# Four small changes of order in a two-block kernel on one core: rounds, weights, swap tiles, taps

## The chip, the cores and the metric

The kernel runs on one core of a Trainium2 chip. The metric is the device time of one execution in microseconds. The core has five engines with a queue each: TensorE (PE, matmuls; its weight loads are PEld), VectorE (DVE), ScalarE (ACT), GpSimd (POOL) and SyncE (SP), which here only issues DMAs. They meet at semaphores; each engine runs its instructions in the order in which they were written.

## The reference

Two blocks on 1024 tokens of width 1024, in float32. The first block has two layers. Each: a norm; `z = hn @ w_in` (256 columns for a pooling mixer, then queries, keys and values of 12 heads of 64); a rotary turn of the first 16 of each head's 64 features; attention in three patterns of window and dilation, whose outputs are weighed by a softmax over their log sums; `w_out`; an FFN of width 4096 with a squared ReLU; a gated addition. The second block (`hybrid_layer`) is one layer:

```python
q, k, v, z_att, glu_a, glu_b, z_conv, g_att, g_conv = split(x @ w_in + b_in)
att_branch = (stick_breaking_attention(q, k, v) * silu(z_att)) @ w_att_proj
c = glu_a * sigmoid(glu_b)
c = silu(layer_norm(causal_depthwise_conv(c, conv_w, conv_b)))   # 31 taps, 512 channels
conv_branch = (c * silu(z_conv)) @ w_conv_proj + b_conv_proj
merged = sigmoid(g_att) * att_branch + sigmoid(g_conv) * conv_branch
y = layer_norm(ALPHA * x + merged @ w_out)
```

Stick breaking: the weight of key s for query t is `sigmoid(z)` times the product of `1 - sigmoid(z)` over all later keys before t, a running product along the keys.

## The kernel before, in words

Everything lies with features on partitions and tokens along the free axis, in two halves of 512 tokens. Each float32 product is three matmuls of rounded operands (`triple`, L1248 to L1250): high by high, low by high, high by low. The weights of a linear layer come in panels of 128 output features and 8 chunks of 128 input features. SP loads a panel into one of two slots of `w_raw` (`load`), POOL splits it into `w_hi` and `w_lo` (`split`, four operations, two for each half of the chunks), and PE runs it for both halves of the tokens (`half`, `half2`; 24 matmuls each). The first four halves of a layer run panel 0 and panel 1 on the first tokens, then both on the second. The order of work on every engine is written out by hand; side jobs are woven between PE's chunks by tables (`weave`, `weave2`), which put a job behind chunk k of half m.

**Start of a layer.** Panels 0 and 1 are the pooling input. PE then sums squares over features with a matmul by ones (L1298), ACT takes a root into `rstd`, DVE inverts it. POOL clears the rope tables and `swapped_rows` (`prepare`, L1087 to L1089; in layer 0 not before ACT has squared ten tiles), then SP loads the rope tables. Before the change, POOL's order is split 0, split 1, `prepare`, split 2, `attention_consts`, split 3. `PANELS` is 108 per layer.

**The rotary turn** (`take_qk`, `add_swapped`, `swap`). There are 6 units of a query, a key and a value panel. For each half of a query or key panel DVE writes bank times cosine to `q_t` or `k_t` (L2266) and bank times sine to the one tile `s_half` (L2270, which frees the bank); SP sends four small DMAs (L859, L860) from `s_half` to `swapped_rows`, with the two groups of eight rows exchanged; DVE adds `swapped_rows` (L2257). The add of one half stands ahead of the next write of `s_half`, so that the tile is free. The value panel goes to `v_feat` (L2277), in front of the last add; PE transposes it (`turn_v`, L1304) behind chunk 1 of the next unit's first half.

**Stick breaking** (`score`, `scan`, `turn_weights`, `meet`). Four pairs of heads, 12 rounds each of up to 512 keys (`ROUNDS`), and three steps more for lagging work. A round: PE scores (L1596), ACT makes `fail` and `weight` (L2075, L2076), POOL masks the diagonal, DVE scans (L2662, L2664) and multiplies (L2669), PE transposes two steps later (L1583), ACT copies, and PE multiplies by the values (`meet`, L1570). The rounds of pairs 0 to 2 stand 4 chunks apart, those of the last pair, beside the four panels of `z_att` (Z_ATT), 3 chunks. `take_z` gates the attention output, with `s_half` as its tile; `lower_weighed` splits it.

**The convolution** (`convolve`) is 124 taps on DVE (L2617, L2621), each a multiply and add over 1024 tokens. They are put between other work on DVE: one beside some of the rounds, eleven behind the last `lower_weighed`, and up to ten behind each gate panel of G_ATT.

**Gate panels** (`panel2`). From G_ATT on, a panel runs both halves into one of two pairs of banks; a panel of 8 chunks (a gate: ACT's `gate`, L2109, frees the bank) takes turns with one of 4 chunks (a projection: DVE's product, L2754, frees it). Four panels of Z_CONV lie between G_ATT and G_CONV; `branch_high` and `branch` prepare the convolution branch there.

Of the kernel before, what the change touches and what calls it, by code (L numbers as in the profile page):

```python
# [10 lines left out]
ALU = mybir.AluOpType  # L11
ACT = mybir.ActivationFunctionType

P = 128
# [50 lines left out]
def half_bank_no(no):  # L65

    l, m = divmod(no, HALVES)
    if l < DEPTH and m >= GATE_AT:
        return (6, 7, 0, 1, 2)[(24 * BLOCKS + m - GATE_AT) % 5]  # L70
    return (0, 1, 2, 6, 7)[m % 5] if m < (10 if l < DEPTH else 20) else m % 3
# [223 lines left out]
GLU, QKV, Z_ATT, G_ATT, Z_CONV, G_CONV, W_OUT2, PANELS2 = 0, 8, 20, 24, 40, 44, 60, 68  # L295
# [7 lines left out]
PAIRS = 4  # L303
# [18 lines left out]
def weave2():  # L322
    at = {}

    def put(m, k, *job):
        at.setdefault(m, []).append((k, job))

    put(0, 1, "stat", 0)
    put(1, 3, "stat", 1)
    for c in range(PAIRS):  # L330
        m0 = 2 * QKV + 6 * (c + 1)
        for b in range(2):

            k = 6 + b if c == PAIRS - 1 else 8 + b
            put(m0 + k // 8, k % 8, "turn_v2", c, b)
        for u in range(STEPS2 if c == PAIRS - 1 else len(ROUNDS)):
            k = 2 + (3 if c == PAIRS - 1 else 4) * u
            put(m0 + k // 8, k % 8, "stick", c, u)
    for m in at:
        at[m].sort(key=lambda x: x[0])  # L340
    return at
# [58 lines left out]
def two_blocks(nc, x, p, positions, norm1, w_in, pool_w, pool_scale, w_out, norm2, w_up, w_down,  # L400
# [39 lines left out]
    tmp = place("tmp", [P, HALF])  # L440
# [136 lines left out]
    ple_raw_loaded = sem("ple_raw_loaded")  # L577
    tables_stored = sem("tables_stored")
    rope_loaded = sem("rope_loaded")
    rows_swapped = sem("rows_swapped")  # L580
    spilled = [sem(f"spilled{k}") for k in range(KC)]
    reloaded = [sem(f"reloaded{k}") for k in range(KC)]
    stats_out = sem("stats_out")
# [129 lines left out]
    w_out2_d = w_out_2[0].rearrange("(k q) f -> q k f", q=P)  # L713

    ALL = DEPTH * PANELS
    ROTATIONS = 4 * UNITS
    STATS = 6

# [8 lines left out]
    def half_cols(hf):  # L727
        return slice(hf * HALF, hf * HALF + HALF)
# [69 lines left out]
    def _(sp):  # L798
# [55 lines left out]
        def swap(l, n, hf):  # L854

            sp.wait_ge(half_free, half_no(l, n, hf) + 1)
            cols = half_cols(hf)
            for at in (0, 64):
                sp.dma_start(swapped_rows[at:at + 8, cols], s_half[at + 8:at + 16]).then_inc(rows_swapped, 16)  # L859
                sp.dma_start(swapped_rows[at + 8:at + 16, cols], s_half[at:at + 8]).then_inc(rows_swapped, 16)  # L860

        def read_stats(l, c):
            sp.wait_ge(stats_out, 64 * (2 * l + c + 1))
# [100 lines left out]
    def _(pool):  # L964
# [164 lines left out]
        for l in range(DEPTH):  # L1129
            for n in range(PANELS):  # L1130
                if n in (GATE - 2 * UP + 3, GATE - 2 * UP + 5):
                    for c in range(2):
                        lower_p(l, c, (n - GATE + 2 * UP) // 2 - 1)
                if is_pair(l * PANELS + n):
                    split_pair(l * PANELS + n)
                elif l or n >= 2:
                    split(l * PANELS + n)
                if n == 1:
                    prepare(l)
                if n == 2:  # L1140
                    attention_consts(l)
                if 4 <= n < 10:
                    mixing(l, n - 4)
                if n >= GATE:
                    split_ple(l, n - GATE)
# [588 lines left out]
    def _(act):  # L1734
# [370 lines left out]
        def gate(m, col, func, dst=gate2[:]):  # L2105
            if m > G_ATT:
                act.wait_ge(slot_free, m - G_ATT)
            act.wait_ge(panel_done, m - G_ATT + 1)
            a.activation(dst, ring[m % 2][:], func, bias=bias2[:, col:col + 1]).then_inc(slot_free, 1)  # L2109
# [22 lines left out]
        for k in range(4):  # L2132
            act.wait_ge(ln_step, LN_SCALED1 + k)
            a.activation(conv_out[:, k], conv_out[:, k], ACT.Silu, scale=conv_par[:, 1, k:k + 1], bias=conv_par[:, 2, k:k + 1]).then_inc(ln_silued, 1)
        for f in range(4):
            if f >= 2:
                gate(Z_CONV + f, 24 + f, ACT.Silu, conv_in[:, f])
            branch_high(f)
        def merged_high(k):

# [24 lines left out]
    def _(dve):  # L2165
        v = nc.vector
# [84 lines left out]
        def add_swapped(l, unit, i, hf):  # L2251
            r, g = rotation(l, unit, i, hf), unit % GROUPS
            dst = half_pattern((q_t, k_t)[i][unit % 2][:], g, hf)
            dve.wait_ge(rows_swapped, 64 * (r + 1))
            dve.wait_ge(swap_cleared, l + 1)
            dve.wait_ge(scaled, r + 1)
            v.tensor_tensor(dst, dst, half_tokens(swapped_rows[:, half_cols(hf)], g), ALU.add).then_inc(rotated, 1)  # L2257

        def take_qk(l, unit, i, hf):
            no, g, cols = half_no(l, 2 + 3 * unit + i, hf), unit % GROUPS, half_cols(hf)  # L2260
            if unit < 2 and hf == 0:
                dve.wait_ge(spilled[2 + 3 * unit + i], 16 * (l + 1))
            if unit == 0 and i == 0:
                dve.wait_ge(roped, 4 * l + 2 * hf + 2)
            dve.wait_ge(half_done, no + 1)
            v.tensor_tensor(half_pattern((q_t, k_t)[i][unit % 2][:], g, hf), half_tokens(bank[half_bank_no(no)], g), half_tokens(rope_c[:, cols], g), ALU.mult)\  # L2266
                .then_inc(scaled, 1)
            if i or hf:
                add_swapped(l, unit, (2 * i + hf - 1) // 2, (2 * i + hf - 1) % 2)
            v.tensor_tensor(s_half[:], bank[half_bank_no(no)], rope_s[:, cols], ALU.mult).then_inc(half_free, 1)  # L2270

        def take_v(l, unit, hf):
            no, g, cols = half_no(l, 4 + 3 * unit, hf), unit % GROUPS, half_cols(hf)
# [409 lines left out]
        def take_z(f, hf):  # L2683
            no, cols, at = half2_no(Z_ATT + f, hf), half_cols(hf), 2 * f + hf
            dve.wait_ge(z_gated, at + 1)
            v.scalar_tensor_tensor(s_half[:], bank[half_bank_no(no)], bias2[:, 12 + f:13 + f], s_half[:], ALU.add, ALU.mult).then_inc(half_free, 1)
            dve.wait_ge(half_free, no + 1)
            dve.wait_ge(att_taken, 4 * f + 4)
            v.tensor_tensor(att2[:, f, cols], att2[:, f, cols], s_half[:], ALU.mult).then_inc(att_weighed, 1)
            if at:  # L2690
                lower_weighed(at - 1)
# [6 lines left out]
        for m in range(QKV, G_ATT):  # L2698
            for hf in range(2):
                for _, job in WEAVE2.get(2 * m + hf, ()):  # L2700
                    if job[0] == "stick":
                        if job[2] < len(ROUNDS):
                            scan(*job[1:])
                        c, u = job[1:]
                        if u < len(ROUNDS) and ROUNDS[u][2] == P or c < PAIRS - 1 and u in (1, 2):
                            convolve(1)
                if m < Z_ATT:
                    c, i = divmod(m - QKV, 3)
                    take_qkv(c, i, hf)
                    convolve(3 if c == 0 else 1 if i == 2 and hf else 0)  # L2710
                else:
                    take_z(m - Z_ATT, hf)
        lower_weighed(2 * PAIRS - 1)
        convolve(11)

        def branch(m, f, src, source):
            dve.wait_ge(slot_free, m - G_ATT + 1)
# [146 lines left out]
```

## Time and profile before

| | us |
|---|---|
| median of 3 runs (lowest, highest) | 3215.99 (3215.17, 3216.70) |
| the profiled execution's own time | 3214.32 |
| its span, first to last instruction | 3212.6 |
| PE busy | 3171.4 (99%) |
| DVE busy | 2030.2 (63%) |
| POOL busy | 1725.6 (54%) |
| ACT busy | 988.2 (31%) |
| mean granted clock of PE, share of full | 0.996 |

Busy time is the union of an engine's instructions. PE's matmuls overlap each other: one of 512 columns takes 390 ns in the profile and the next starts 227 ns after it. So what counts is when a matmul starts, and how long PE had no matmul before it.

### The profile page before, as it was taken

How to read it: one execution, taken by the hardware profiler on the slowest of the kernel's cores; microseconds unless marked ns; L12 is line 12 of the kernel's file. 1: busy time of each engine (PE TensorE's matmuls, PEld its weight loads, DVE VectorE, ACT ScalarE, POOL GpSimd, SP SyncE). 2: the span in 40 equal slices, each digit the busy share in tenths (PEclk: the TensorE clock that was granted, in tenths of full speed). 3: DMA queues.
4: the chain of work that ended last, by engine and by line, in shares of the span. 5: the costliest groups of instructions: out<-in, count | busy, mean ns of one | idle time of the engine just before them, and what ended most of it. 6: DMA issues, size and time to landing. Idle time of an engine off the chain costs nothing.

```text
span 3212.6 us, 39393 instructions
## 1 busy us (share of the span) xinstructions
PE 3171.4 (99%) x14756; PEld 2508.2 (78%) x14756; DVE 2030.2 (63%) x2749; ACT 988.2 (31%) x1847; POOL 1725.6 (54%) x1544
## 2 busy tenths in 40 slices
PE   8999999999999999999999999999999999999999
PEld 6676788888888887776788888888888766778887
DVE  6546576666666664545476666665758988797323
ACT  3222243333333421222253333332422244402212
POOL 5632356666666446532356666666455533386575
PEclk9999999999999999999999999999999999999999
DMA  5111211111112121111231111112111100011112
GB/s 151 48 40 34 84 55 53 53 53 53 55 50 63 50 87 55 45 40 45 71 58 53 53 53 53 55 53 66 45 46 46 40 27 27 21 46 50 49 54 85
DMA packets 306349, 173.73 MB, mean 54 GB/s; under 512 B 61424, under 2 KB 296944, under 8 KB 306160
## 3 DMA queue, kind: packets, MB, share of 16 engines
q1 hardware_dynamic: 287904, 162.55, 17.5%
q10 hardware_dynamic: 18256, 8.67, 0.9%
q8 instruction: 118, 1.93, 0.2%
q14 instruction: 71, 0.58, 0.1%
HBM read 155.13 MB, written 12.91 MB: 52 GB/s over the span
## 4 chain that ended last, share of the span: by engine, by line
PE 57%; DVE 2%; ACT 1%; issue 0%; POOL 0%; DMA 0%; SPq 0%; DVEq 0%; ACTq 0%; POOLq 0%
PE ring L1248 11%; PE ring L1249 11%; PE ring L1250 11%; PE aux L1248 3%; PE aux L1250 3%; PE aux L1249 3%; PE ring L1490 2%; PE ring L1491 2%; PE ring L1489 2%; PE aux L1596 1%; PE aux L1490 1%; PE aux L1489 1%; PE aux L1491 1%; PE aux L1570 1%; PE aux L1342 1%; PE aux L1328 1%
## 5 line engine op out<-in xcount | busy, mean ns | idle before, releaser
L996 POOL TENSOR_TENSOR w_hi<-w_raw,ones 128x512 fp32r<-128x512 f32 (+3 forms) x408 | 455.1, 1115 | 905.3 <-PE ring L1250 718.6
L999 POOL TENSOR_TENSOR w_lo<-w_raw,w_hi 128x512 fp32r<-128x512 f32 (+3 forms) x408 | 543.7, 1333 | 32.0
L1248 PE MATMUL ring<-Q_hi,w_hi 128*128 128x512 f32 x1312 | 519.8, 396 | 4.7 <-POOL w_lo L999 3.5
L1249 PE MATMUL ring<-Q_lo,w_hi 128*128 128x512 f32 x1312 | 511.8, 390 | 0.0
L1250 PE MATMUL ring<-Q_hi,w_lo 128*128 128x512 f32 x1312 | 511.7, 390 | 0.0
L1248 PEld LDWEIGHTS ring<-Q_hi,w_hi 128*128 128x128 f32 x1312 | 246.6, 188 | 82.2 <-issue 28.0
L1250 PEld LDWEIGHTS ring<-Q_hi,w_lo 128*128 128x128 f32 x1312 | 246.7, 188 | 52.1
L1249 PEld LDWEIGHTS ring<-Q_lo,w_hi 128*128 128x128 f32 x1312 | 246.8, 188 | 50.3 <-issue 1.0
L1248 PE MATMUL ring<-P_hi,w_hi 128*128 128x512 f32 x656 | 276.5, 422 | 1.2 <-DVE P_lo L2210 1.2
L1250 PE MATMUL ring<-P_hi,w_lo 128*128 128x512 f32 x656 | 257.7, 393 | 0.0
L1249 PE MATMUL ring<-P_lo,w_hi 128*128 128x512 f32 x656 | 257.7, 393 | 0.0
L1248 PE MATMUL aux<-Q_hi,w_hi 128*128 128x512 f32 x544 | 213.3, 392 | 0.0
L1250 PE MATMUL aux<-Q_hi,w_lo 128*128 128x512 f32 x544 | 211.8, 389 | 0.0
L1249 PE MATMUL aux<-Q_lo,w_hi 128*128 128x512 f32 x544 | 211.7, 389 | 0.0
L1933 ACT ACTIVATE aux<-tmp 128x512 f32<-128x512 f32 x112 | 67.4, 602 | 402.0 <-DVE tmp L2386 402.0
L2621 DVE SCALAR_TENSOR_TENSOR conv_out<-conv_in,taps,conv_out 128x1021 f32<-128x1021 f32 (+29 forms) x120 | 186.7, 1607 | 0.2
L1248 PEld LDWEIGHTS ring<-P_hi,w_hi 128*128 128x128 f32 x656 | 124.2, 189 | 48.6 <-issue 21.3
L1250 PEld LDWEIGHTS ring<-P_hi,w_lo 128*128 128x128 f32 x656 | 124.0, 189 | 27.9
L1249 PEld LDWEIGHTS ring<-P_lo,w_hi 128*128 128x128 f32 x656 | 124.5, 190 | 24.3 <-issue 2.9
L2284 DVE COPY probs_t<-aux 128x256 f32<-128x256 f32 (+1 forms) x96 | 52.4, 546 | 141.3 <-PE aux L1328 141.3
L1851 ACT ACTIVATE probs<-probs,neg_max 128x128 f32<-128x128 f32 (+1 forms) x192 | 85.1, 444 | 175.6 <-DVE neg_max L2296 175.6
L1023 POOL TENSOR_TENSOR w_lo<-w_sums,w_hi 128x1024 fp32r<-128x1024 f32 x56 | 134.5, 2401 | 0.0
(396 smaller groups left out, 7059.3 us busy)
## 6 DMA issues: line engine op xcount, KB each, us to landing
w_raw<-in_w_in SPq DMA_DIRECT2D x84, 512.0 KB, 3.8
w_raw<-in_w_up SPq DMA_DIRECT2D x64, 512.0 KB, 4.0
w_raw<-in_w_down SPq DMA_DIRECT2D x64, 512.0 KB, 3.4
h_scratch<-h ACTq DMA_DIRECT2D x16, 512.0 KB, 3.8
w_raw<-in_w_gate SPq DMA_DIRECT2D x16, 512.0 KB, 3.8
hx<-h_scratch SPq DMA_DIRECT2D x12, 512.0 KB, 6.5
x_raw<-in_x SPq DMA_DIRECT2D x8, 512.0 KB, 7.8
w_raw<-in_w_out SPq DMA_DIRECT2D x16, 256.0 KB, 2.9
```

The costliest lines, as they stand in the source:

```text
L996: g.tensor_tensor(w_hi[:, slot, ks], w_raw[:, slot, ks], one.broadcast_to([P, width, P]), ALU.mult).then_inc(w_hi_ready, 1)
L999: g.tensor_tensor(w_lo[:, slot, ks], w_raw[:, slot, ks], w_hi[:, slot, ks].bitcast(F32), ALU.subtract).then_inc(w_ready, 1)
L1023: g.tensor_tensor(w_lo[:, slot], w_sums[:, slot], w_hi[:, slot].bitcast(F32), ALU.subtract).then_inc(w_ready, 1)
L1248: t.matmul(o, wh, xh, start=first, stop=False)
L1249: t.matmul(o, wh, xl, start=False, stop=False)
L1250: return t.matmul(o, wl, xh, start=False, stop=last)
L1489: t.matmul(to[at], wh, xh, start=(i == 0 and not joins), stop=False, skip_group_check=True)
L1490: t.matmul(to[at], wh, xl, start=False, stop=False, skip_group_check=True)
L1491: mm = t.matmul(to[at], wl, xh, start=False, stop=(i == 1), skip_group_check=True)
L1851: a.activation(x_, x_, ACT.Exp, scale=SCALE, bias=neg_max[:, j % 2, e:e + 1], accum_out=row_stat[:, unit, j, 2 + e:3 + e]).then_inc(exped, 1)
L1933: a.activation(square_bank, tmp[:], ACT.Square).then_inc(squared, 1)
L2621: v.scalar_tensor_tensor(conv_out[:, c, shift:], conv_in[:, c, 0:S - shift], tap, conv_out[:, c, shift:], ALU.mult, ALU.add)\
```

## The change

Five edits. In `weave2` the last pair's rounds stand 4 chunks apart, as the others. On POOL `prepare` moves from behind split 1 to behind split 2. For unit 0 the second half's sine product goes to `tmp`, each half has its own semaphore `rows_swapped`, and the add stands behind the next sine product. ACT runs the gate of panel Z_CONV + 2 in front of the two first `branch_high`. Eight of the eleven taps behind `lower_weighed` move: one to round 7 of pairs 0 to 2, three to the last steps of the last pair, two behind `take_z` of the first two Z_ATT panels.

```diff
@@ weave2
-            k = 6 + b if c == PAIRS - 1 else 8 + b
+            k = 8 + b
             put(m0 + k // 8, k % 8, "turn_v2", c, b)
         for u in range(STEPS2 if c == PAIRS - 1 else len(ROUNDS)):
-            k = 2 + (3 if c == PAIRS - 1 else 4) * u
+            k = 2 + 4 * u
@@ two_blocks
-    rows_swapped = sem("rows_swapped")
+    rows_swapped = [sem(f"rows_swapped{hf}") for hf in range(2)]
+    def rotation_tile(unit, hf):
+        return tmp if unit == 0 and hf else s_half
@@ SP, swap
-            cols = half_cols(hf)
+            cols, scaled_half = half_cols(hf), rotation_tile((n - 2) // 3, hf)
             for at in (0, 64):
-                sp.dma_start(swapped_rows[at:at + 8, cols], s_half[at + 8:at + 16]).then_inc(rows_swapped, 16)
-                sp.dma_start(swapped_rows[at + 8:at + 16, cols], s_half[at:at + 8]).then_inc(rows_swapped, 16)
+                sp.dma_start(swapped_rows[at:at + 8, cols], scaled_half[at + 8:at + 16]).then_inc(rows_swapped[hf], 16)
+                sp.dma_start(swapped_rows[at + 8:at + 16, cols], scaled_half[at:at + 8]).then_inc(rows_swapped[hf], 16)
@@ POOL
-                if n == 1:
+                if n == 2:
                     prepare(l)
-                if n == 2:
                     attention_consts(l)
@@ ACT, behind the four Silu of the convolution branch
+        gate(Z_CONV + 2, 26, ACT.Silu, conv_in[:, 2])
         for f in range(4):
-            if f >= 2:
-                gate(Z_CONV + f, 24 + f, ACT.Silu, conv_in[:, f])
+            if f == 2:
+                gate(Z_CONV + 3, 27, ACT.Silu, conv_in[:, 3])
             branch_high(f)
@@ DVE, add_swapped
-            dve.wait_ge(rows_swapped, 64 * (r + 1))
+            dve.wait_ge(rows_swapped[hf], 64 * (r // 2 + 1))
@@ DVE, take_qk
-            if i or hf:
+            if unit and (i or hf):
                 add_swapped(l, unit, (2 * i + hf - 1) // 2, (2 * i + hf - 1) % 2)
-            v.tensor_tensor(s_half[:], bank[half_bank_no(no)], rope_s[:, cols], ALU.mult).then_inc(half_free, 1)
+            v.tensor_tensor(rotation_tile(unit, hf)[:], bank[half_bank_no(no)], rope_s[:, cols], ALU.mult).then_inc(half_free, 1)
+            if unit == 0 and (i or hf):
+                add_swapped(l, unit, (2 * i + hf - 1) // 2, (2 * i + hf - 1) % 2)
@@ DVE, stick breaking and behind it
-                        if u < len(ROUNDS) and ROUNDS[u][2] == P or c < PAIRS - 1 and u in (1, 2):
+                        if u >= len(ROUNDS) or ROUNDS[u][2] == P or c < PAIRS - 1 and u in (1, 2, 7):
                             convolve(1)
...
                     take_z(m - Z_ATT, hf)
+                    if hf and m - Z_ATT < 2:
+                        convolve(1)
         lower_weighed(2 * PAIRS - 1)
-        convolve(11)
+        convolve(3)
```

## Rows read from the trace of the kernel before

**Rows 1.** PE's waits, whole run: line, releaser, us in total, times, longest.
```profile
PE ring L1304 <- DVE v_feat L2277: 9.9, 2, 5.0
...
PE aux L1248 <- POOL w_lo L999: 5.0, 1, 5.0
PE aux L1583 <- DVE weight L2669: 3.6, 4, 2.4
PE ring L1248 <- POOL w_lo L999: 3.5, 1, 3.5
PE ring L1248 <- ACT conv_in L2109: 1.2, 1, 1.2
```

**Rows 2.** Stretches: length, busy of PE, PEld, DVE, ACT, POOL, clock, DMA, GB/s.
```profile
47.00:52.00 5.00, 4.58 (x14) 3.67 (x15) 4.22 (x7) 3.38 (x6) 4.46 (x8) 0.66 0.96 351
89.00:95.00 6.00, 5.93 (x18) 4.96 (x19) 1.05 (x1) 0.71 (x2) 5.84 (x5) 0.51 0.14 28
...
2768.00:2780.00 12.00, 8.70 (x52) 6.42 (x52) 9.13 (x9) 4.38 (x8) 1.19 (x1) 1.00 0.08 23
...
2815.00:2820.00 5.00, 4.77 (x14) 3.79 (x15) 5.00 (x3) 0.00 (x0) 4.92 (x4) 0.66 0.00 0
...
1278.00:1284.00 6.00, 5.43 (x20) 4.55 (x21) 1.53 (x2) 0.91 (x2) 5.43 (x5) 0.60 0.12 23
```

**Rows 3.** Timeline, PE in layer 0: start, length, operation, [idle before, releaser].
```profile
47.42 0.77 PE L1248 MATMUL aux<-P_hi,w_hi 128*128 128x512 f32 x1 [5.03 <-POOL w_lo L999]
...
57.84 1.02 PE L1298 MATMUL ring<-sumsq,ones 128*128 128x512 f32 x2
```

**Rows 4.** Timeline, POOL in layer 0: first clearing, last `w_lo` of panel 2.
```profile
42.20 0.96 POOL L1087 MEMSET rope_s<- 128x1024 f32 x1 [21.16 <-ACT aux L1770]
...
48.35 1.29 POOL L999 TENSOR_TENSOR w_lo<-w_raw,w_hi 128x512 fp32r<-128x512 f32 x1
```

**Rows 5.** Timeline, DVE in layer 0: last add of squares.
```profile
51.77 0.69 DVE L2205 TENSOR_TENSOR sumsq<-aux,sumsq 128x512 f32<-128x512 f32 x1 [0.26 <-ACT aux L1770]
```

**Rows 6.** Timeline, DVE in layer 1: rotary turn of unit 0.
```profile
1259.81 0.67 DVE L2270 TENSOR_TENSOR s_half<-aux,rope_s 128x512 f32<-128x512 f32 x1
...
1264.53 0.69 DVE L2257 TENSOR_TENSOR q_t<-q_t,swapped_rows 128x512 f32<-128x512 f32 x1 [3.45 <-DMA swapped_rows<-s_half]
...
1277.16 1.27 DVE L2277 TENSOR_TENSOR v_feat<-aux,rstd 128x512 f32<-128x512 f32 x2
```

**Rows 7.** Timeline, SP in layer 1: the load behind the first swap.
```profile
1263.22 0.44 SPq L847 DMA_DIRECT2D w_raw<-in_w_in  x1
```

**Rows 8.** Timeline, PE in layer 1: sum of squares, first transposes.
```profile
1247.47 1.02 PE L1298 MATMUL ring<-sumsq,ones 128*128 128x512 f32 x2
...
1278.57 1.08 PE L1304 MATMUL ring<-ident,v_feat 128*128 128x128 f32 x4 [4.87 <-DVE v_feat L2277]
```

**Rows 9.** Last pair: PE's longest wait; two stretches, last pair, pair before.
```profile
2771.68 0.66 PE L1583 MATMUL aux<-ident,weight 128*128 128x128 f32 x4 [2.42 <-DVE weight L2669]
...
2718.00:2776.00 58.00, 54.53 (x307) 36.25 (x307) 52.43 (x51) 35.30 (x61) 21.57 (x17) 1.00 0.08 23
...
2655.00:2717.00 62.00, 61.84 (x341) 42.54 (x341) 51.01 (x47) 30.62 (x54) 25.20 (x20) 1.00 0.09 26
```

**Rows 10.** Timeline, gate panels of G_ATT: DVE, POOL and PE.
```profile
2799.86 13.08 DVE L2621 SCALAR_TENSOR_TENSOR conv_out<-conv_in,taps,conv_out 128x1011 f32<-128x1011 f32 x11
...
2923.03 1.21 DVE L2754 TENSOR_TENSOR merged<-ring,gate 128x1024 f32<-128x1024 f32 x1
...
2806.46 7.37 POOL L996 TENSOR_TENSOR w_hi<-w_raw,ones 128x512 fp32r<-128x512 f32 x1 [7.67 <-PE ring L1250]
...
2844.46 1.10 POOL L996 TENSOR_TENSOR w_hi<-w_raw,ones 128x512 fp32r<-128x512 f32 x1 [4.39 <-PE ring L1250]
...
2925.75 0.39 PE L1248 MATMUL ring<-branch_hi,w_hi 128*128 128x512 f32 x1
```

**Rows 11.** Timeline, ACT: the second copy of the convolution branch.
```profile
2977.45 1.06 ACT L2113 ACTIVATE branch_hi<-conv_out 128x1024 fp32r<-128x1024 f32 x1 [3.43 <-DVE conv_out L2718]
```

## The prediction

> **What bounds the kernel.** I read the list of who waited for whom on TensorE first. TensorE (PE) is the engine that is nearly always busy in the profile's table, so a change can only win where PE stands still, or runs slowly after it stood still. The list has few lines [rows 1]: PE waits for `v_feat` at the transposes of L1304 (9.9 us, one wait of 5.0 and one of 4.9 in the two layers), once for POOL's weights in the first stage (5.0), four times for DVE's `weight` in stick breaking (3.6), once more for POOL's weights at the start of the gate panels (3.5), once for ACT's gate (1.2). 
>
> **Part 1, third panel's weights in front of the clearing.** In layer 0 POOL stands from 21 to 42.20 for ACT's squares before it may clear the tables, and only then splits panel 2, the last `w_lo` from 48.35 [rows 4]; PE, done with panel 1 at 42.2, restarts at 47.42 [rows 3]. In the new order the split waits only for PE's third half, whose last matmul starts 24 matmuls (5.5 us) and a sum of features (about 1 us) before 42.2, so near 35.5. The split takes what it takes here, 49.6-44.9 = 4.7 us, ends near 41 (42 if DVE's operations hold it), and its first half is ready near 38.5. The wait is gone with its slow stretch: 5.0+1.5 = 6.5 us. What is late next: the second sum of squares (L1298) stands at 57.84 [rows 3] and would now come at 51.3, but DVE's last add of squares ends at 51.77+0.69 = 52.46 [rows 5], and that chain (ACT square, DVE add, in turn) doesn't hang on PE. New wait 1.2 us. Besides, DVE's small angle operations at 39 to 41.5 now lie beside POOL's last `w_lo` (1.3 us): between 0 and 1.3 us later for the whole DVE chain, I take 0.5. Net gain 6.5-1.2-0.5 = 4.8, bounds 4.0 and 5.3. The clearing starts at 42.2 as before, since ACT's squares release it, so the rope loads on SP, and the load of panel 4 behind them, stay where they are; panel 4 is run two panels (four halves of 5.5 us) behind panel 2, from 64 on, and its load, issued by 53 behind the rope tables, and its split of 4.7 us end before that. POOL's constants and the split of panel 3 move up by the 4.7 us. In layer 1 the clearing moves from idle time to behind the split (2.7 us); SP's four rope loads and the load of panel 4 queue behind it and move with it. Nobody on PE's side waits: the tables are first read 6.4 us after L1298, PE needs panel 3 some 10 us later than it is split. Zero, with 0 to 1 us of loss as bounds.
>
> **Part 2, two tiles to swap from.** Today each rotated half is a closed circle: `s_half` at 1259.81, four DMA issues on SP, landing, the add at 1264.53, and only then the next `s_half` [rows 6]; three circles of 4.7 to 5.9 us stand before `v_feat` at 1277.16, done at 1278.4, and PE's transposes start at 1278.57 after 4.9 us of waiting [rows 8], so PE arrived at 1273.6. With a second tile the next product doesn't wait and SP's queue sets the pace: a swap's issues end where SP issues the load of weights behind it, at 1263.22 (0.44 us) [rows 7], 2.7 us after `s_half` was written, and the add follows 1.3 us later. Swap 2 then goes at 1263.7 to 1266.4 and lands at 1267.7; swap 3 goes at 1266.4 to 1269.1 and lands at 1270.5 (its product needs the add at 1264.53 only); DVE adds it until 1271.3 and writes `v_feat` twice, 1.2 us: 1272.5, with 0.14 to PE 1272.7. PE comes at 1273.6. So `v_feat` is ready 0.9 us early and the wait goes whole; swap 4 is added near 1275, and PE needs that some 6 us after its transposes. From L1298 to the transposes PE takes 1273.6-1247.47 = 26.1 us [rows 8] and DVE 25.2, and layer 0 has the same distances since both its chains hang on L1298. Gain in layer 0: 5.0+2.7 (the start-to-start distances behind it give 2.5, the clock row 2.9) = 7.7; in layer 1 4.9+2.0 = 6.9. If every add were stretched by POOL (0.6 to 1.2 us, three of them), 1 us of wait comes back in each layer.
>
> **Part 3, rounds four chunks apart.** All four waits of the 3.6 us lie in the last pair, the longest, 2.42 us, at 2771.68. In its rounds DVE is busy 52.4 of 58 us; in the pair before, with rounds four chunks apart, 51.0 of 62, and PE waits nowhere [rows 9]. A chunk is three matmuls, 0.68 us; over the last pair's twelve steps PE takes 12 of them more, and 3.3 us of waiting less: 58-3.3+8.2 = 62.9 us, for DVE's 52.4 and two moved taps of 1.2: 54.8. That is 87% where the pair before has 82% and no wait. Gain 3.6; at worst 1.5 of it stays. The last meet comes 14 chunks later, in the last half of the stage; `att_ready` is needed 5 chunks and a 10.9 us panel after it, DVE and ACT need about 7: hidden.
>
> **Part 4, taps spread.** Behind the stage DVE runs eleven taps back to back (2799.86, 13.08 us); POOL's `w_hi` starts at 2806.46 inside them and takes 7.37 us, until the taps end [rows 10]; PE waits 3.5 [rows 1]. With three taps (3.6 us) DVE is idle from 2803.5, POOL's split ends at 2806.46+4.7 = 2811.2, its first half at 2808.9, and PE wants it at 2811.7. Gain 3.5+1.6 = 5.1. The eight taps moved (1.2 us each) go into rounds with idle DVE time and to round 7 of three pairs, where two rounds of lag absorb 1.2 us. What is late next: the product `merged` of the seventh gate panel, 2923.03, ends 1.5 us before PE starts the panel that needs its bank at 2925.75 [rows 10]. DVE's tap series restart from PE's fourth panel in both versions, so this slack should stay; I take 0.2 off. 4.9.
>
> The Trainium skill, "SBUF — State Buffer", section "Who interferes with whom", says that a VectorE operation with two SBUF inputs and a GpSimd operation lock each other out for one whole instruction. By that the `w_hi` would have lasted one tap and itself, 2.3 us, and PE wouldn't have waited, so moving taps would win nothing there; the row of 7.37 us says that it was held through six taps, and I go by the row.
>
> **Part 5, ACT's gate for panel Z_CONV+2 earlier.** Now it runs at 2978.4, behind two copies; ahead of the second ACT waits 3.43 us for DVE, from 2974.0 [rows 11], and the gate needs 1.1. Ahead of both copies it is done by 2974, 4 us before PE asks for the bank. Gain 1.2. The first copy slips 0.2 us; its reader comes 10 us later.
>
> **Sum.** 4.8+7.7+6.9+3.6+4.9+1.2 = 29.1. The profiled execution took 3214.3 (span 3212.6 and 1.7 around it), giving 3185.2; it lies 1.7 under the median, so I predict **3187**. If every residue is nothing: 3186.
>
> The Trainium skill, "TensorE: Matmul & The Clock Gate", section "HAM oscillation — how this bites in real kernels", says that a wait can throttle the engine again. The rows agree for waits from 3.5 us and not for 2.4 [rows 2]; if the new wait did it, rival (a2) below is the time.
>
> **Rivals.** (a) As above, 3187, 3184 to 3191: 0.68. (a2) The new wait at L1298 sets the clock back as the four long ones do; it is shorter than the 2.4 us that didn't, but stands on its own: 1.5 us, 3188.5, 0.04. (b) DVE becomes late in the tap series: PE gets ahead of it by the 5.1 us it no longer loses, and the slack of 1.5 us at 2925.75 is eaten; for it, DVE is never idle over five panels there; against it, its series restarts at PE's fourth panel. A wait of 3.6 and 1.6 of slow clock: 3192. 0.10. (c) The swap still binds: the small copies issued behind a 512 KB load land with it, 3 us later than I put them; for it, both share SP's queue; against it, the circles after such a load are no longer today. A wait of 2 to 3 us per layer stays, 3187+5 = 3192. 0.09. (d) The taps don't hold POOL, something else did, or they hold it in another place: the change doesn't do what it says in part 4, 3192. 0.05. (e) Slower. The hold of POOL is not rare but comes whenever a split meets a tap series; five series of ten taps run through the gate panels, and the shifted start lets each meet the split of the next. Each hold costs up to 6.3 us at PE and 1.6 of clock, 7.9; three leave 5 us of the gain, from four on the kernel is slower; all five: 3187+5x7.9 = 3226. For it only the one hold; against it, a split that starts inside a series at 2844.46 takes 1.10 us [rows 10]. 0.02. (f) Small losses in several places, together over 20 us, within 0.2% of no change: 0.02.
>
> **Range.** (a) with (b) to (d): 3183 to 3195 holds over 8 in 10. A measurement here tells about 0.2% (6.4 us) from no change. Faster 0.96 ((a) to (d)), same 0.02 (f), slower 0.02 (e).
>
> **What would show it.** In the list of PE's waits L1304, L1583 and both L1248 lines behind `w_lo` gone, a new one of 1 to 2.5 us at L1298 behind `sumsq`; POOL's clearing in layer 0 still at 42; `v_feat` 1 us ahead of L1304; POOL's `w_hi` at the first gate panel 1.0 us; granted clock 1.00 in all four stretches. Wrong if L1304 still waits over 2 us, or if the gate panels show new waits.

## The result

Four runs of the changed kernel took 3191.18 to 3192.55 us, median **3191.8**; the kernel before took 3216.0 beside them (3215.17 to 3216.70). The ratio is 0.9925 with a 95% interval of 0.9908 to 0.9942: 24.2 us faster, where 29.1 were forecast. 3191.8 lies in the range given (3183 to 3195) and is 4.8 us above the value forecast, 3187. (The change has five parts; the title leaves out the fifth, ACT's gate.) The profiled execution took 3191.67 us (span 3189.9), 22.65 under that of before.

The profile after, first PE's waits (line, releaser, us in total, times, longest), to be read against [rows 1]:

```profile
PE aux L1409 <- DMA x_raw<-in_x: 7.2, 1, 7.2
PE ring L1302 <- DVE sumsq L2210: 3.8, 1, 3.8
PE aux L1587 <- DVE weight L2676: 2.2, 3, 1.7
PE aux L1332 <- ACT probs L1855: 1.6, 3, 1.1
PE ring L1252 <- DVE P_lo L2215: 1.2, 2, 0.7
PE ring L1360 <- DVE weights L2334: 0.6, 2, 0.3
PE ring L1252 <- DVE pool_u L2251: 0.5, 1, 0.5
```

The lines are four further down than before: L1302 was L1298, L1308 was L1304, L1587 was L1583, L1332 was L1328. Gone are the waits for `v_feat` (9.9), both for POOL's `w_lo` (5.0, 3.5) and the one for ACT's gate (1.2). The first line, for x, was there before. Three are over 1 us larger than forecast: 3.8 us at the second sum of squares (1.2 forecast), 2.2 us at L1587 (0 forecast), 1.6 us for `probs` (0.5 before, no change forecast). The clock in the stretches of [rows 2] and behind the new wait (length, busy of PE, PEld, DVE, ACT, POOL, clock, DMA, GB/s):

```profile
47.00:52.00 5.00, 4.54 (x19) 3.12 (x17) 4.54 (x8) 1.95 (x4) 4.68 (x6) 1.00 0.53 142
56.00:60.00 4.00, 4.00 (x10) 2.66 (x10) 1.77 (x1) 1.97 (x2) 0.00 (x0) 0.57 1.07 392
1278.00:1284.00 6.00, 6.00 (x31) 4.30 (x32) 5.59 (x14) 1.38 (x5) 4.95 (x5) 1.00 0.03 6
```

The slow stretches of before are at full clock; one has come in their place, 56 to 60 us at 0.57, which costs (1-0.57)x4 = 1.7 us.

Where the time came from is read from the start of the same matmul in both traces (the n-th matmul of L1248 before and of L1252 after; there are 3200 in each):

| up to | before | after | difference | this part | forecast |
|---|---|---|---|---|---|
| behind the second sum of squares, layer 0 | 60.79 | 60.40 | -0.4 | part 1: 0.4 | 4.8 |
| behind the transposes of `v_feat`, layer 0 | 96.84 | 88.56 | -8.3 | part 2: 7.9 | 7.7 |
| the same in layer 1 | 1292.72 | 1278.62 | -14.1 | part 2: 5.8 | 6.9 |
| behind stick breaking | 2792.55 | 2776.81 | -15.7 | part 3: 1.6 | 3.6 |
| second gate panel | 2819.67 | 2798.58 | -21.1 | part 4: 5.4 | 4.9 |
| last input panel of the convolution | 2979.65 | 2957.15 | -22.5 | part 5: 1.4 | 1.2 |

So of the 6.5 us that are missing between the profiles (29.1 less 22.65) 4.4 lie in part 1, 1.1 in layer 1 and 2.0 in part 3, together 7.5; parts 2 (layer 0), 4 and 5 gave 0.9 more than forecast, and 0.1 came behind the last row. One profile tells such a shift to about 1 us: in four more profiles with the order of before in the first stage (the kernel before with part 3, 4 or 5 alone, and the old order below) the matmul of the first row stands 0.2 to 1.1 us later than 60.79.

**Part 1.** DVE in layer 0 (start, length, operation, count, [idle before, releaser]):

```profile
39.63 1.15 DVE L2188 TENSOR_SCALAR turns<-ang 128x64 f32<-128x64 f32 x1
40.82 0.19 DVE L2190 TENSOR_SCALAR turns<-turns 128x64 f32<-128x64 f32 x1
...
42.32 1.81 DVE L2199 TENSOR_SCALAR turns<-turns 128x64 f32<-128x64 f32 x1
44.16 3.35 DVE L2235 RECIPROCAL rstd<-rstd 128x512 f32<-128x512 f32 x1
...
54.97 0.69 DVE L2210 TENSOR_TENSOR sumsq<-aux,sumsq 128x512 f32<-128x512 f32 x1 [0.75 <-ACT aux L1774]
```

and POOL and PE beside it:

```profile
39.39 1.34 POOL L1004 TENSOR_TENSOR w_lo<-w_raw,w_hi 128x512 fp32r<-128x512 f32 x1
42.23 0.96 POOL L1092 MEMSET rope_s<- 128x1024 f32 x1 [1.50 <-ACT aux L1774]
43.12 0.96 POOL L1093 MEMSET rope_c<- 128x1024 f32 x1
```

```profile
55.81 1.31 PE L1302 MATMUL ring<-sumsq,ones 128*128 128x512 f32 x2 [3.81 <-DVE sumsq L2210]
```

An operation of 0.19 us takes 1.15 and ends at 40.78, as POOL's `w_lo` ends (40.73); another takes 1.81 and ends at 44.13, as the second memset ends (44.08). The first pushed the second into the clearing, which DVE had been through with before. The last add of squares ends at 55.66; before it was 52.46 [rows 5].

**Layer 1.** PE doesn't wait for `v_feat`, but 1.1 us for `probs`. DVE, POOL and PE:

```profile
1273.45 2.40 DVE L2303 TENSOR_SCALAR neg_max<-row_stat 128x2 f32<-128x2 f32 x1
```

```profile
1273.43 2.39 POOL L1076 TENSOR_TENSOR pool_u<-mix,pool_u 128x1024 f32<-128x1024 f32 x1
```

```profile
1276.82 0.44 PE L1332 MATMUL aux<-ident,probs 128*128 128x128 f32 x2 [1.13 <-ACT probs L1855]
```

The same scaling of two numbers per row takes 0.17 us elsewhere. PE has come nearer to DVE by the wait it lost, and what stood in the shadow of that wait now stands in its way: with the wait back (one tile, below) PE waits 0.5 us for `probs`, as before.

**Part 3.** The end of the last pair in DVE, then POOL and PE:

```profile
2746.92 2.04 DVE L2628 SCALAR_TENSOR_TENSOR conv_out<-conv_in,taps,conv_out 128x1010 f32<-128x1010 f32 x1
2748.88 3.43 DVE L2671 TENSOR_TENSOR_SCAN left<-fail,not_yet 128x512 f32<-128x512 f32 x2
...
2762.96 3.91 DVE L2669 TENSOR_TENSOR_SCAN left<-fail,left 128x511 f32<-128x511 f32 x2 [0.23 <-DVE weight L2676]
2767.00 1.78 DVE L2676 TENSOR_TENSOR weight<-weight,left 128x1024 f32<-128x1024 f32 x1
```

```profile
2761.60 2.02 POOL L1159 TENSOR_TENSOR w_hi<-w_raw,ones 128x512 fp32r<-128x512 f32 x1 [3.03 <-PE ring L1254]
...
2767.78 2.13 POOL L1162 TENSOR_TENSOR w_lo<-w_raw,w_hi 128x512 fp32r<-128x512 f32 x1
```

```profile
2768.84 0.66 PE L1587 MATMUL aux<-ident,weight 128*128 128x128 f32 x4 [1.71 <-DVE weight L2676]
```

From the tap to the product at 2767.00 DVE is idle for no more than 0.23 us at a time, between its own operations. The scans at 2762.96 lie beside POOL's split of the output weights and take 3.91.

### The profile page after: what moved, and what is told of

It is laid out like the page before. It is cut to its first block, busy times and chain, and to the rows that moved or that the text cites. A ratio compares the mean times of both kernels' runs of the same rounds, so it can differ in the third digit from the quotient of the medians.

```text
span 3189.9 us, 39393 instructions
## 1 busy us (share of the span) xinstructions
PE 3164.3 (99%) x14756; PEld 2503.5 (78%) x14756; DVE 2036.2 (64%) x2749; ACT 988.1 (31%) x1847; POOL 1719.1 (54%) x1544
## 4 chain that ended last, share of the span: by engine, by line
PE 95%; DVE 4%; ACT 1%; issue 0%; DMA 0%; DVEq 0%; ACTq 0%; SPq 0%
PE ring L1252 18%; PE ring L1254 17%; PE ring L1253 17%; PE aux L1252 5%; PE aux L1254 5%; PE aux L1253 5%; PE ring L1495 3%; PE ring L1494 3%; PE ring L1493 3%; PE aux L1493 2%; PE aux L1494 2%; PE aux L1495 2%; PE aux L1346 1%; PE aux L1332 1%; PE aux L1322 1%; PE aux L1600 1%
## 5 line engine op out<-in xcount | busy, mean ns | idle before, releaser
L1001 POOL TENSOR_TENSOR w_hi<-w_raw,ones 128x512 fp32r<-128x512 f32 (+3 forms) x408 | 448.3, 1099 | 917.4 <-PE ring L1254 735.5
L1252 PE MATMUL ring<-Q_hi,w_hi 128*128 128x512 f32 x1312 | 519.2, 396 | 0.0
L1252 PEld LDWEIGHTS ring<-Q_hi,w_hi 128*128 128x128 f32 x1312 | 246.2, 188 | 76.4 <-issue 26.3
L1252 PE MATMUL ring<-P_hi,w_hi 128*128 128x512 f32 x656 | 275.8, 420 | 1.6 <-DVE P_lo L2215 1.2
L1252 PE MATMUL aux<-Q_hi,w_hi 128*128 128x512 f32 x544 | 213.3, 392 | 0.0
L1252 PEld LDWEIGHTS ring<-P_hi,w_hi 128*128 128x128 f32 x656 | 123.4, 188 | 49.3 <-issue 21.3
```

Source lines behind the costliest of these rows:

```text
L1001: g.tensor_tensor(w_hi[:, slot, ks], w_raw[:, slot, ks], one.broadcast_to([P, width, P]), ALU.mult).then_inc(w_hi_ready, 1)
L1252: t.matmul(o, wh, xh, start=first, stop=False)
```

## The experiments

All of them were timed in five rounds against the kernel before. Three base kernels occur: the one before, the changed one, and the changed one with the angles early. The median of the kernel before was 3215.0 to 3216.1 us in the four sets of runs, so a difference between times of two sets is good to about 1 us.

**Where part 1 went.** The angle operations moved into a gap of DVE, from 20 us:

```
             lower(P_hi, P_lo, gains[:, 0, 0], KC - 1, hf, KC * hf + KC - 1)
+            if hf == 0:
+                angles()
         for k in range(KC):
...
-        angles()
         for l in range(DEPTH):
```

> The changed kernel (3191.8 us) with DVE's ten small angle operations moved from behind the first sum of squares (39.1 to 44.1 us of the span) to the gap between the two halves of x (from 20 us). Theory: the 4.8 us that the third panel's weights were to bring were lost because the one-input ones among them stood until POOL's operation in flight was over (1.15 and 1.81 us for 0.20 each), and the chain behind them made TensorE wait 3.8 us for sumsq and then run 3.4 us at the half clock. Then the reciprocal starts at about 41 and not 44.2, the wait for sumsq falls from 3.8 to 0.5 to 1.2, the low clock behind it goes, and the time is 3186 to 3188. Rival 1: the squares are held back by ACT's own issues of the spills (1.6 and 1.5 us long), whatever comes before: the wait falls by 1 us at most, 3190 to 3191. Rival 2: the ten operations hold the second half of P back and TensorE with it: 3192 or more.

Measured 3187.12 (3185.65 to 3187.46), ratio 0.9912 (0.9898 to 0.9925), 4.7 us under the changed kernel, with no run of the one inside the other's. Its waits, one row of DVE, one of PE, one stretch:

```profile
PE aux L1587 <- DVE weight L2677: 2.2, 3, 1.7
PE ring L1252 <- DVE P_lo L2215: 1.2, 2, 0.7
PE aux L1332 <- ACT probs L1855: 1.1, 2, 0.8
PE ring L1302 <- DVE sumsq L2210: 0.9, 1, 0.9
```

```profile
40.92 3.35 DVE L2237 RECIPROCAL rstd<-rstd 128x512 f32<-128x512 f32 x1 [1.94 <-ACT rstd L1786]
```

```profile
52.02 1.10 PE L1302 MATMUL ring<-sumsq,ones 128*128 128x512 f32 x2 [0.94 <-DVE sumsq L2210]
```

```profile
56.00:60.00 4.00, 4.00 (x19) 3.31 (x18) 3.96 (x6) 0.00 (x0) 0.00 (x0) 1.00 0.54 151
```

The reciprocal starts 3.24 us earlier, the wait is 0.9 where 3.8 stood, and the clock behind it is full (from 52 to 56 us too). That is 2.9 us of waiting and 1.7 of slow clock less, and the matmul of the table's first row starts at 55.02, 5.8 us ahead of the kernel before, where part 1 was to bring 4.8. The theory holds; ACT's issues were no bound.

The old order of clearing and split, in the changed kernel:

```
-                if n == 2:
+                if n == 1:
                     prepare(l)
+                if n == 2:
                     attention_consts(l)
```

> The changed kernel with the clearing of the tables in front of the third panel's split again (part 1 undone, all else kept). Theory (from the shifts of TensorE's matmuls, 0.2 us behind the first stage): part 1 as it stands gives 0.2 us in layer 0, and it costs 1.1 us of waiting for probs in layer 1, where a maximum's scaling lies beside another operation of POOL; so the time is 3191 to 3192.5. Rival: part 1 gives the 4.8 us that were forecast and something else lost them: 3196 to 3197.

Measured 3192.38 (3191.73 to 3193.33), ratio 0.9929 (0.9915 to 0.9942): 0.6 us over the changed kernel, less than two sets tell apart, and far from the rival's 3196. Part 1 as it stands gives next to nothing. The wait for `w_lo` is back (5.0) and that for `sumsq` gone. The second half of my expectation fell: the waits for `probs` are 1.6 us here too, so they don't come from part 1.

**What holds DVE's small operations.** The factor of the row maxima from a tile (on the kernel with the angles early):

```
-            v.tensor_scalar(neg_max[:, s % 2], row_stat[:, unit, s, 0:2], -SCALE, None, ALU.mult)
+            v.tensor_tensor(neg_max[:, s % 2], row_stat[:, unit, s, 0:2], small[:, 5:6].broadcast_to([P, 2]), ALU.mult)
```

> The kernel of angles_early (3187.1 us) in which the scaling of the row maxima (128x2, 96 times) takes its factor from a tile (two inputs, tensor_tensor) and not as a constant (one input, tensor_scalar). In the profile of the changed kernel 15 of the 96 take up to 2.40 us for 0.17, each until POOL's operation in flight ends. Theory: only the one-input form is held by POOL. Then all 96 take 0.17 to 0.4 us, the waits for probs (1.1 us) fall to under 0.4, and the time is 3186.0 to 3187.0. Rival: any small operation of DVE is held that starts inside one of POOL's: again some 14 of the 96 above 0.5 us, the time stays at 3187.

Measured 3186.52 (3186.30 to 3187.78), ratio 0.9914 (0.9900 to 0.9927): no change that can be told, and the theory fell. 14 of the 96 are held over 0.25 us longer than the shortest, as with the angles early (15 in the changed kernel), each to the end of one of POOL's operations; the longest takes 1.61 us. The group in the two kernels, the one with the angles early first (line, operation, count, busy us, mean ns, idle before):

```profile
L2305 DVE TENSOR_SCALAR neg_max<-row_stat 128x2 f32<-128x2 f32 x96 | 24.7, 257 | 3.3
```

```profile
L2308 DVE TENSOR_TENSOR neg_max<-row_stat,small 128x2 f32<-128x2 f32 x96 | 24.4, 255 | 3.3
```

Both forms, with all operands in SBUF, are held. The Trainium skill, "SBUF — State Buffer", section "Who interferes with whom", says that `tensor_scalar` can take the port pair that it shares with GpSimd, that `tensor_tensor` with both inputs in SBUF contends with GpSimd's reads, and that the one to come later is blocked for the whole instruction. These rows agree with it for both forms. The 1.81 us in layer 0 go beyond it: they last through two memsets, and not one.

**Part 2.** One tile again, in the changed kernel:

```
-        return tmp if unit == 0 and hf else s_half
+        return s_half
...
-            if unit and (i or hf):
+            if i or hf:
                 add_swapped(l, unit, (2 * i + hf - 1) // 2, (2 * i + hf - 1) % 2)
```

and the later add taken out.

> The changed kernel (3191.8) with one tile to swap the first unit's rows from again (part 2 undone). Theory: the two waits for v_feat of 5 us and the slow stretches behind them come back, 7.9 and 6.9 us by the shifts: 3205.5 to 3206.6. Rival: with the third panel's weights in time and sumsq late, the swaps stand otherwise and only one of the waits comes back: 3198 to 3200.

Measured 3203.43 (3201.95 to 3204.45), ratio 0.9965 (0.9952 to 0.9977): 11.6 us over the changed kernel (12.8 between the profiled executions), between the two expectations.

```profile
PE ring L1308 <- DVE v_feat L2282: 8.0, 2, 5.0
...
PE ring L1302 <- DVE sumsq L2210: 3.7, 1, 3.7
```

In layer 0 the wait is 3.0 and not 5.0: behind the late sum of squares PE ran at half clock (0.50 from 57 to 61 us) and lost about 2 us of its lead over DVE. In layer 1 it is 5.0. The clock falls behind both:

```profile
89.00:94.00 5.00, 5.00 (x20) 4.07 (x19) 1.09 (x1) 1.12 (x2) 4.84 (x5) 0.66 0.12 23
1277.00:1282.00 5.00, 4.83 (x18) 4.05 (x18) 1.07 (x2) 0.60 (x1) 4.84 (x5) 0.57 0.13 26
```

**Part 3.** Undone in the changed kernel, and alone on the kernel before (the same two lines the other way):

```
-            k = 8 + b
+            k = 6 + b if c == PAIRS - 1 else 8 + b
...
-            k = 2 + 4 * u
+            k = 2 + (3 if c == PAIRS - 1 else 4) * u
```

> The changed kernel with the last pair's rounds three chunks apart again (part 3 undone). Theory: part 3 was worth 1.6 us by the shifts (waits for weight 3.6 down to 2.2), since POOL's split of the output weights now falls beside the last scans: 3193 to 3194. Rival: it was worth 3.6 us as forecast: 3195.4. Rival: with the moved taps among rounds three apart DVE is later still and the part is worth more than forecast: 3197 or more.

> The kernel before with part 3 alone: the last pair's rounds four chunks apart, no tap moved. Theory: without the moved taps the waits for weight fall from 3.6 to 0.7 (as in taps_at_the_end), a gain of 2.9; the eleven taps behind the last round start later against TensorE and the product merged becomes late as there, up to 5.1 us of waits, in the place of POOL's hold (3.5 and 1.6): 3212.5 to 3214. Rival: the hold of POOL stays as before and merged is in time: 3212.4 to 3213. Rival: both, hold and lateness: 3216 or more.

Undone: 3195.47 (3194.43 to 3197.17), ratio 0.9939 (0.9927 to 0.9952), 3.7 us over the changed kernel; the waits for `weight` are 4.6, one of them 3.6, with the clock at 0.50 behind it (2759 to 2764 us). Alone: 3212.80 (3211.99 to 3213.20), ratio 0.9990 (0.9981 to 0.9999), 3.3 us under the kernel before; the waits are 0.7. So the part is worth the 3.6 us of the forecast, by the second expectation; the 1.6 in the table is what is left after the moved taps, with which the waits there are 1.5 longer (0.7 without them, 2.2 with them).

**Part 4.** Undone in the changed kernel, and alone on the kernel before:

```
-                        if u >= len(ROUNDS) or ROUNDS[u][2] == P or c < PAIRS - 1 and u in (1, 2, 7):
+                        if u < len(ROUNDS) and ROUNDS[u][2] == P or c < PAIRS - 1 and u in (1, 2):
                             convolve(1)
...
-                    if hf and m - Z_ATT < 2:
-                        convolve(1)
...
-        convolve(3)
+        convolve(11)
```

> The changed kernel with the eleven taps behind the last round again and none of the eight moved ones (part 4 undone). Theory: the taps hold POOL's split again, TensorE waits 3.5 us and runs slowly for 1.6: 4.9 to 5.6 us more, 3196.7 to 3197.4, less up to 1.5 if the tap in the last rounds is part of what makes TensorE wait for weight there. Rival: with the rounds four apart POOL's split no longer meets the taps: 3191 to 3192.

> The kernel before (3216.0) with part 4 alone: eight taps spread, three behind the last round. Theory: POOL's 7.37 us w_hi and the wait of 3.5 with its slow stretch go (5.1), the moved taps make DVE later in the last pair's rounds, three chunks apart (the waits for weight were 4.6 in three_apart, 3.6 before: 1.0): 3211.4 to 3212.4. Rival: since the taps at the end did not hold POOL in taps_at_the_end (1.38 us for its w_hi) but made the product merged late by 5.1 us in all, the part also takes such lateness away and is worth more here: under 3210.5. Rival: without the shift of the rounds nothing is won: 3215 to 3216.

Undone: 3196.08 (3195.04 to 3197.76), ratio 0.9941 (0.9929 to 0.9954), 4.3 us over. Alone: 3210.45 (3209.60 to 3211.39), ratio 0.9983 (0.9974 to 0.9992), 5.6 us under; its waits for `weight` are 4.6 (3.6 before), and the clock is at 0.66 behind the longest (2772 to 2777 us). Both sizes are near the 4.9 forecast, but the way is another. POOL and PE's waits with the taps at the end:

```profile
2804.75 1.38 POOL L1001 TENSOR_TENSOR w_hi<-w_raw,ones 128x512 fp32r<-128x512 f32 x1 [2.94 <-PE ring L1254]
```

```profile
PE ring L1252 <- DVE merged L2761: 5.1, 4, 2.3
PE ring L1302 <- DVE sumsq L2210: 3.3, 1, 3.3
...
PE aux L1587 <- DVE weight L2676: 0.7, 1, 0.7
```

POOL isn't held; DVE's product `merged` is late, four times, 5.1 us in all. Is that the new order, or was the 7.37 us of [rows 10] a chance of that one execution? Part 5 alone on the kernel before leaves everything ahead of 2975 us as it was:

```
+        gate(Z_CONV + 2, 26, ACT.Silu, conv_in[:, 2])
         for f in range(4):
-            if f >= 2:
-                gate(Z_CONV + f, 24 + f, ACT.Silu, conv_in[:, f])
+            if f == 2:
+                gate(Z_CONV + 3, 27, ACT.Silu, conv_in[:, 3])
```

> The kernel before with part 5 alone (ACT's gate for the third value panel ahead of both copies). Nothing ahead of 2975 us differs from the kernel before. Theory: the wait of 1.2 us at that panel goes: 3214.6 to 3215.0. And a second look at the place where POOL's w_hi took 7.37 us beside DVE's taps, with the same order of work: if it takes 7 us again, it belongs to this order; if it takes 1 to 2 us, it is chance between executions, and PE's wait of 3.5 us there is gone in this profile too. Rival: the gate's time is hidden anyway, 3216.

Measured 3214.65 (3212.96 to 3215.25), ratio 0.9995 (0.9986 to 1.0004): 1.4 us, as the shift of part 5, though the interval holds no change too. Its waits, and POOL where it was held before:

```profile
PE ring L1304 <- DVE v_feat L2278: 9.9, 2, 5.1
...
PE ring L1248 <- DVE merged L2755: 5.1, 4, 2.3
PE aux L1248 <- POOL w_lo L999: 5.0, 1, 5.0
PE aux L1583 <- DVE weight L2670: 3.7, 4, 2.4
```

```profile
2805.92 1.48 POOL L996 TENSOR_TENSOR w_hi<-w_raw,ones 128x512 fp32r<-128x512 f32 x1 [7.67 <-PE ring L1250]
2807.47 2.13 POOL L999 TENSOR_TENSOR w_lo<-w_raw,w_hi 128x512 fp32r<-128x512 f32 x1
```

PE behind the last of these waits, and the clock there:

```profile
2925.94 0.47 PE L1248 MATMUL ring<-branch_hi,w_hi 128*128 128x512 f32 x1 [2.33 <-DVE merged L2755]
```

```profile
2926.00:2931.00 5.00, 5.00 (x15) 3.97 (x16) 4.93 (x3) 0.95 (x1) 4.92 (x3) 0.66 0.00 0
```

With the same order of work, POOL takes 1.48 us where it took 7.37, and the 3.5 us wait for `w_lo` isn't there; the 5.1 us for `merged` are. In one execution DVE went first through all its taps, and POOL stood; in the other they took turns (POOL's longer operations 2.0 to 2.1, most taps 2.0 to 2.3 us), and DVE came late. Why the turns failed once isn't known; of the fourteen profiles of this case (four of them with eleven taps there) no other has an operation of POOL over 2.6 us in this stage or behind it.

The two ways don't cost the same. By the starts of the same matmuls between the end of stick breaking and the last gate panels, against the profiles with the taps spread (part 4 alone, the changed kernel), the hold costs 5.4 us (3.5 of waiting, 1.6 of slow clock, the rest at the restart). The turns cost 7.8 in this profile and in the one of taps at the end (5.1 of waiting in four waits, 1.7 of slow clock behind the last, the rest at the restarts), and 7.1 with part 3 alone, where the clock stays full and PE waits 0.6 more at L1669. The spread taps in turn cost 2.5 us up to the end of stick breaking with part 4 alone: there it is 1.0 us ahead of the kernel before at the matmul of 1292.72 and 1.4 behind it at that of 2792.55. 7.8 less 2.5 is 5.3, beside the 5.6 measured.

**What is left in the last pair.** POOL's split held until the last product is made; one tap put back; both (on the kernel with the angles early):

```
+                    if m == QKV + 3 * PAIRS + 3 and steps == 0:
+                        pool.wait_ge(z_weighed, PAIRS * len(ROUNDS))
                     if steps in (0, 2):
```

```
-                    if hf and m - Z_ATT < 2:
+                    if hf and m == Z_ATT:
                         convolve(1)
...
-        convolve(3)
+        convolve(4)
```

> The kernel of angles_early with POOL's split of the output weights behind the last rounds waiting until DVE's last product weight is made, so that it lies beside none of the last scans. Theory: the last wait of 1.7 us at L1587 comes from this split (the last scans take 3.91 us beside it where 2.46 do without, the product 1.78 for 1.23): both get short, the wait goes, 3185.4. The panel that needs this split comes some 8 us later, the split takes 4.7. Rival 1: DVE was late before that already, from the tap before the scans: the wait falls by less than 0.5, 3186.7 to 3187.2. Rival 2: the split is late for its panel, a new wait for w_lo: 3188 or more.

> The kernel of angles_early with one of the eight moved taps (the one behind the fourth gated half, 19 us ahead of the 1.7 us wait at L1587) put back behind the rounds: four taps there and not three. Theory: DVE has no idle time from this tap to the product that TensorE waits for, so each microsecond of it (it takes 2.0) is one of the wait: the wait goes, and the fourth tap at the end costs nothing: 3185.4. Rival: the wait comes from POOL's split beside the last scans alone: it stays at 1.0 to 1.7, 3186.5 to 3187.1. Rival: four taps at the end are one too many, the product merged is late again: over 3188.

> The kernel of angles_early (3187.1 us) with both late_split and tap_later. Theory: in the last pair DVE's lateness is the sum of the tap and of POOL's split beside the last scans, and either alone took only 1.0 to 1.5 of the 2.2 us of waits; together the waits at L1587 fall to under 0.5, and the time is 3184.3 to 3185.3. Rival: the 0.7 us that late_split left are not DVE's lateness in the last rounds but stand elsewhere: 3185.3 to 3185.8, no better than either.

| | median (range) | ratio (95%) | waits at L1587 |
|---|---|---|---|
| angles early | 3187.12 (3185.65 to 3187.46) | 0.9912 (0.9898 to 0.9925) | 2.2 |
| and late split | 3185.69 (3184.65 to 3185.82) | 0.9910 (0.9896 to 0.9923) | 0.7 |
| and tap later | 3185.25 (3184.42 to 3185.67) | 0.9909 (0.9896 to 0.9923) | 1.2 |
| and both | 3185.29 (3184.77 to 3186.06) | 0.9905 (0.9892 to 0.9919) | 0.5 |

The last scans with the late split, and with the tap later:

```profile
2759.04 2.46 DVE L2672 TENSOR_TENSOR_SCAN left<-fail,left 128x511 f32<-128x511 f32 x2 [0.23 <-DVE weight L2679]
2761.63 1.23 DVE L2679 TENSOR_TENSOR weight<-weight,left 128x1024 f32<-128x1024 f32 x1
```

```profile
2755.73 3.90 DVE L2670 TENSOR_TENSOR_SCAN left<-fail,left 128x511 f32<-128x511 f32 x2 [0.23 <-DVE weight L2677]
2759.76 1.78 DVE L2677 TENSOR_TENSOR weight<-weight,left 128x1024 f32<-128x1024 f32 x1
```

The scans take 2.46 without POOL and 3.9 beside it: the split is one cause of the wait, the tap another; each mend takes 1.0 to 1.5 us of the waits off. Both together bring the waits to 0.5 but no time beyond either: in that profile the wait for `sumsq` is 1.5 and those for `probs` 1.5, which are 0.9 and 1.1 with the angles early; differences of half a microsecond between these kernels are not told apart by the times. All three are faster than both kernels of the case, by some 30 and 6 us.

## Why the prediction was right, and where it wasn't

- **The reading of the bound** held: what was won were waits of PE and the slow clock behind them, and the stretches behind the four long waits of [rows 2] are at full clock. Two slips change nothing in the forecast: the five waits add up to 23.2 and not 24.4 (the bound to 31), and that a wait of 2.4 us leaves the clock full is no rule: it fell behind 2.3 us in two other profiles.
- **Part 1, wrong.** The step that failed is the one on DVE's angle operations, "between 0 and 1.3 us later for the whole DVE chain, I take 0.5". It counted the length of POOL's last `w_lo` as the bound and left out what comes next: a chain pushed back by 1 us meets the clearing, where another operation is held for 1.6 us more. Together 2.7 us at the reciprocal (44.16 for 41.46), 3.2 at the last square, and behind the wait of 3.8 us the clock falls. Rival (a2) was thus what came. Its 1.5 us for the clock measured 1.7; what was too small is the wait itself, 3.8 us where the sum has 1.7 (1.2 and 0.5). Together that is 3.8 of the 4.4 us lacking; the rest is within what one profile tells. The run with the angles early shows it by moving only these operations.
- **Part 2, right** in layer 0 (7.9 for 7.7). In layer 1 5.8 for 6.9: `v_feat` is ready in time, but 1.1 us come back at the next reader, `probs`. The prediction's "what is late next" looked at the swaps alone. The angles-early profile has a wait of 0.8 without the hold at 1273.45, but with another: from a scaling held for 1.32 us at 1281.40 and an add that takes 2.67 at 1283.67 DVE has no gap up to the scaling at 1288.25, for which ACT, and through it PE, waits. That it is these two, no run shows.
- **Part 3.** Its 3.6 was right (3.7 undone, 3.3 alone). Wrong was that the moved taps are free there because DVE is busy 87% and not 100%. That share is a mean over rounds; in the last ones DVE had no idle time, and the moved taps made the waits 1.5 longer; taking one of them away took 1.0 off.
- **Part 4, the number right** (4.3 undone, 5.6 alone, 4.9 forecast) **for the wrong reason.** The hold of POOL was read from one execution and is not what the eleven taps cost in the three other profiles that have them; there DVE is late, four times. Rival (b), DVE late in the series, didn't come in the changed kernel, where no gate panel waits; it is what the kernel before does in the second look. Rival (e) didn't come. The number is luck in part: the eleven taps cost 7.8 us and not 5.1, and the moved ones were not free in the last pair. The 2.3 us for `w_hi` that the prediction set aside for the row of 7.37 was nearer to the other three profiles (1.38 to 1.48), but its conclusion, that moving taps wins nothing, was wrong as well, since DVE pays for the turns.
- **The base.** The forecast starts from a profiled execution 1.7 us under its median and adds the 1.7 again. The changed kernel's profile lies only 0.15 under its median, so 22.65 us between the profiles are 24.2 between the medians, which hides part of the miss. That the profile of before went the cheaper of the two ways would account for it; which way the other executions went is not shown.
- **Part 5, right**: 1.4 for 1.2.
- Rivals (c) and (f) didn't come; (d) was half true in its mechanism, since in three of four profiles the taps didn't hold POOL, and false in its time.

## What to carry to other kernels

A short operation can cost what is running beside it when it starts, and not its own length: before another engine's work is moved, list the small operations that will lie under it, and then those that their delay pushes under the next one. A mean share of busy time says nothing of a deadline: follow DVE's chain back from the wait that is to vanish and see whether it has a gap. And an odd duration in one profile (7.37 us) is worth a second profile of the same code before a step of an argument stands on it.

## What the runs showed of the hardware

- An operation of DVE on 128x2 numbers, 0.17 us long, took up to 2.40 us, until the operation of POOL beside which it started was done (1.61 us at most with two inputs from SBUF, 2.40 with one). A memset of POOL, which only writes, held a one-input operation as well: 1.81 us for 0.20, through two memsets.
- In three of the four profiles with eleven taps behind the rounds, DVE and POOL, both at work on SBUF, took turns operation by operation (a tap 2.0 to 2.3 us for 1.25 alone, POOL's `w_hi` 2.0 for 1.04); in the fourth POOL stood through six of DVE's in a row.
- The length of a wait alone doesn't say whether TensorE's clock falls behind it. Behind every wait of 3.0 us or more inside the run it fell to the lower level for part of the stretch: 3.0 (one tile, 0.66 over 89 to 94 us), 3.3 (taps at the end, 0.58 over 56 to 60), 3.8 (changed kernel, 0.57). Of waits of 2.3 to 2.4 us it fell behind two (part 5 alone, 0.66 over 2926 to 2931; taps at the end, 0.66 over 2908 to 2913) and stayed full behind three (2.42 before; 2.43 with part 5 alone; 2.33 with part 3 alone, 1.00 over 2923 to 2928). Behind the 7.2 us with which every run begins it is full.
